# Copies with a factor, rotated products and raw latent tiles: out of PSUM by ScalarE or by VectorE

## The chip, the cores and the metric

The kernel runs on one core of a Trainium2 chip. Time is device time in microseconds; before the change the median of three runs is 1549.19 us (1547.57 to 1551.87). A separate execution was recorded by the hardware profiler, and all rows below come from it.

## The reference

A network of two different blocks, each of two layers, on 512 tokens of width 1024, all in float32. Cut to what matters:

```python
# block 1, each layer: h = x @ w_in, cut into the inputs of four branches
q  = rms_norm(c_q, q_norm) @ w_qb;  kv = rms_norm(c_kv, kv_norm) @ w_kvb      # mla: latents of rank 384 and 256
y_mla = softmax(causal(rope(q) k^T / sqrt(96))) v
y_sb  = stick_breaking(sq * d**-0.5, sk, sv)     # a[t,s] = sigmoid(z[t,s]) * prod_{s<j<t}(1 - sigmoid(z[t,j]))
y_fox = softmax(causal(fq * d**-0.5 . fk) + cumulated log forget gates) fv
y_mem = softmax((mem_q * d**-0.5) mk^T) mv                                    # keys and values from mem
merged = sum_n sigmoid(merge_r @ w_up)_n * ((y_n * silu(gate_n)) @ w_branch_n)
x = layer_norm(4**0.25 * x + merged @ w_out)
# block 2, each layer: h = rms_norm(x), z = h @ w_in_2, four attentions
q_a, k_a = axial_rope(rms_norm(q_a)), axial_rope(rms_norm(k_a))               # A: dense
q_b, k_b = rope(q_b), rope(k_b)                                               # B: window of 128, sink
o_c = neighbourhood(q_c, k_c, v_c, bias)                                      # C: 8x16 neighbourhood
q_d, k_d = rope(q_d), rope(k_d)                                               # D: difference of two softmaxes
x = x + concat(o_n * silu(g_n)) @ w_out_2
```

## The kernel before

There are five instruction streams (TensorE, VectorE, ScalarE, GpSimd, SyncE) that meet only at semaphores. A planner, `plan`, writes one list of steps. Each engine walks through the whole list in its order and takes from each step what is its own, so each engine's queue is the order of that list. A wait in a queue holds everything behind it on that engine.

**Matrix products.** Each is done in three passes for accuracy: a float32 operand is split into a high and a low part, and low x high, high x low and high x high are added in PSUM (L1399, L1400, L1401, one k-tile of 128 at a time). Weights of about 1 MB are loaded by DMA into one of two buffers, cast by ScalarE in pieces of 512 columns to the high part (L1552), and the low part is subtracted by VectorE (L1861) or GpSimd (L2296). The planner puts such a piece of the next weights in (`tick`) after every few k-tiles.

**Fill and main.** The planner interleaves two strands (`alongside`): the attention of one branch (main) and the projections of the next branch (fill). While mem's attention runs, mla's latents are projected; under mla's attention sb, under sb's fox, under fox's most of the merge. In the second block A is projected alone, then B under A's attention, D under B's, C under D's. So TensorE's order alternates between logits (L1421, L1427, L1439), transposes of the probabilities (L1455, L1464), probabilities times values (L1477), and k-tiles of projections.

**Attention.** Per chunk of two heads and 128 queries: logits into PSUM; VectorE takes the maximum (L2092, L2128) or adds the mask with it (L2105); ScalarE's exponential with the row sum (L1533, the line of a helper for every ACTIVATE with a function); TensorE transposes; the first half of the turned probabilities is copied by VectorE (L2165), the second by ScalarE (L1755); then the product with the values, the gate by VectorE (L2186), cast by ScalarE (L1767). The stick-breaking branch has sigmoids on ScalarE and scans and products on VectorE (L2151, L2154, L2157). D subtracts two softmaxes on VectorE (L2136 to L2141).

**Latents of mla.** Five tiles of 128 channels x 512 tokens (three of the query, two of the key and value latent) are computed, copied to SBUF raw (step `raw`, for the fourth `rawcopy`) by VectorE at L1958, and squared by ScalarE. TensorE sums the squares over channels (L1488), ScalarE makes the root (Ln, Exp), VectorE refines it by a Newton step (`newton_wide`, L1824 to L1830) and scales the tiles (L1968); ScalarE casts them (L1628), GpSimd makes the low part (L2310). The norm of the first three tiles (step `normed`) stands in the list behind the fifth tile's `raw`.

**Heads.** A branch that isn't rotated gets its queries by step `head` with part q: bank x 0.125 into SBUF, by VectorE at L1935, for fox in two halves of 64 partitions at L1932. There are two such steps (chunks c = 0, 1) per layer for each of mem, sb, fox and C. The keys (part k) are copied by ScalarE already (L1592, L1586).

**Rotated branches.** For A, B and D step `pair` copies each of three tiles (two of queries, one of keys) with its factor to SBUF (L2197 on VectorE; for A the factor is a column of gains). For A, ScalarE waits for this copy and then squares the same bank. Some k-tiles later TensorE multiplies the copy by a rotation matrix (L1508, step `rope2`), for A also the squares by a block of ones (L1516, step `qsquares`). VectorE combines copy and rotated product with the tables (L2208 to L2216), and for A refines the root and normalises (L1824 to L2224).

Of the kernel before, what the change touches and what calls it, by code (L numbers as in the profile page):

```python
# [1109 lines left out]
def build(nc, ctx, a, out):  # L1110
# [177 lines left out]
    def tensor_program(e):  # L1288
# [33 lines left out]
        def heads_ready(l, br):  # L1322
            if br == "mem":
                w.wait_ge(v_copy, v_copy.at(("head", l, br, "q", 1)))
                w.wait_ge(a_copy, a_copy.at(("mkv", l, 0, 1)))
                w.wait_ge(v_copy, v_copy.at(("mkv", l, 1, 1)))
            elif br == "mla":
                w.wait_ge(v_fn, v_fn.at(("rope1", l, "q")))
                w.wait_ge(v_copy, v_copy.at(("qnope", l, 1)))
                w.wait_ge(a_copy, a_copy.at(("mlav", l, 3)))  # L1330
            elif br in PAIRED:
                w.wait_ge(v_fn, v_fn.at(("paired", l, br, 2)))
                w.wait_ge(v_copy, v_copy.at(("vturn", l, br)))
            else:
                if br == "fox":
                    w.wait_ge(v_fn, v_fn.at(("foxrow", l, 3)))
                w.wait_ge(v_copy, v_copy.at(("value", l, br, 2)))
                w.wait_ge(a_copy, a_copy.at(("value", l, br, 3)))

        for s in STEPS:  # L1340
# [162 lines left out]
            elif k == "rope2":  # L1503
                b = s["b"]
                for g, v in b.free():
                    w.wait_ge(g, v)
                w.wait_ge(v_copy, v_copy.at(("pair", s["src"])))
                t = e.matmul(bank(b), C(ROT[s["br"]][0]), tm(s["src"]), start=True, stop=True)  # L1508
# [20 lines left out]
    def scalar_program(e):  # L1529
# [5 lines left out]
        for s in STEPS:  # L1535
# [37 lines left out]
            elif k == "spread":  # L1573
                for l in range(2):
                    w.wait_ge(d_z, d_z.at("z"))
                    src = zrow[:, l, :].unsqueeze(1).to_broadcast([60, 64, P])
                    e.dma_start(zscr[l], src).then_inc(d_spread.sem, d_spread.mark("z"))
            elif k == "head" and s["part"] == "k":
                l, br, c, b = s["l"], s["br"], s["c"], s["b"]
# [25 lines left out]
            elif k == "mkv" and s["n"] == 0:  # L1605
# [4 lines left out]
                t = e.copy(mk[:, c, :], bank(b)[:, 0:256])  # L1610
                t.then_inc(a_copy.sem, a_copy.mark(("mkv", l, 0, c), ends=(b,)))
            elif k in ("raw", "rawsquare"):
                w.wait_ge(v_copy, v_copy.at(("raw", s["l"], s["n"])))
                for g, v in s["tm"].free():
# [143 lines left out]
            elif k == "out":  # L1758
# [57 lines left out]
    def vector_program(e):  # L1816
# [35 lines left out]
        for s in STEPS:  # L1852
# [45 lines left out]
            elif k == "lambdas":  # L1898
# [10 lines left out]
                for l in range(2):  # L1909
# [9 lines left out]
                        v_fn.sem, v_fn.mark("lambdas"))  # L1919
            elif k == "head" and s["part"] == "q":  # L1920
                l, br, c, b = s["l"], s["br"], s["c"], s["b"]
                dst = QKV[br][0]
                w.wait_ge(gemm, gemm.at(b))
                if br in BEFORE:
                    w.wait_ge(heado, heado.at(("heado", l, BEFORE[br], 1)))
                if br == "sb":
                    w.wait_ge(y_lo, y_lo.at(("normed", l, 4)))
                if br == "fox":
                    w.wait_ge(p_fn, p_fn.at(("zeros", l)))
                    for half in range(2):  # L1930
                        p0 = 64 * half
                        t = e.tensor_scalar(dst[p0:p0 + 64, 2 * c + half, :], bank(b)[p0:p0 + 64, :], 0.125, None, ALU.mult)  # L1932
                        t.then_inc(v_copy.sem, v_copy.mark(("head", l, br, "q", c), ends=(b,)))
                else:
                    t = e.tensor_scalar(dst[:, c, :], bank(b), 0.125, None, ALU.mult)  # L1935
                    t.then_inc(v_copy.sem, v_copy.mark(("head", l, br, "q", c), ends=(b,)))
            elif k == "value" and s["i"] % 2 == 0:
# [11 lines left out]
            elif k == "mkv" and s["n"] == 1:  # L1949
# [5 lines left out]
                t.then_inc(v_copy.sem, v_copy.mark(("mkv", l, 1, c), ends=(b,)))  # L1955
            elif k in ("raw", "rawcopy"):
                w.wait_ge(gemm, gemm.at(s["b"]))
                t = e.tensor_copy(raw(s["n"]), bank(s["b"]))  # L1958
                t.then_inc(v_copy.sem, v_copy.mark(("raw", s["l"], s["n"]), ends=(s["b"],)))
            elif k == "normed":  # L1960
# [219 lines left out]
            elif k == "out":  # L2180
# [6 lines left out]
                t.then_inc(v_fn.sem, v_fn.mark(("gated", ta), ends=(b, s["u"])))  # L2187
            elif k == "pair":
                l, br, n, b = s["l"], s["br"], s["n"], s["b"]
                gain = 1.0 if n == 2 else {"A": None, "B": 0.125, "D": float(32 ** -0.5)}[br]  # L2190
                if br == "A":
                    gain = pcol(f"kna{l}") if n == 2 else qna8[:, l:l + 1]
                w.wait_ge(gemm, gemm.at(b))
                w.wait_ge(v_fn, v_fn.at("lambdas"))
                for g, v in s["tm"].free():
                    w.wait_ge(g, v)
                t = e.tensor_scalar(tm(s["tm"]), bank(b), gain, None, ALU.mult)  # L2197
                t.then_inc(v_copy.sem, v_copy.mark(("pair", s["tm"]), ends=(b,)))
            elif k == "rope2":
# [283 lines left out]
```

## Time and profile before

| | |
|---|---|
| median of three runs | 1549.19 us (1547.57 to 1551.87) |
| the profiled execution | 1553.94 us |
| its span | 1552.0 us, 21224 instructions |
| mean granted TensorE clock in it | 0.97 |
| moved copies, VectorE | 48 instructions: 12 of L1935, 8 of L1932, 10 of L1958, 18 of L2197 |

The span runs from the first to the last instruction of the profiled execution. A row of the time line has the start, the duration, the engine, the line, what is written from what; "[3.12 <-ACT prob L1755]" says that the engine had been idle for 3.12 us before this instruction and that the last thing it waited for was ScalarE's instruction at L1755. PE is TensorE, DVE VectorE, ACT ScalarE. Layers 0 and 1 of a block show the same pattern of waits, 416 to 426 us apart in the first block and 344 us in the second.

### The profile page before, as it was taken

The page shows a single profiled execution, that of the slowest core. Times are in us where ns is not written, and L with a number is a line of the kernel's source. Part 1 is how long each engine was busy: PE and PEld are TensorE (multiplying, and loading weights), DVE is VectorE, ACT ScalarE, POOL GpSimd, SP SyncE. Part 2 cuts the span into 40 slices and gives each one's busy share as a digit, 9 for nine tenths or more (in the row PEclk, how much of TensorE's full clock was granted, in tenths as well). Part 3 has the DMA queues.
Part 4 walks back from the last instruction along what each step waited for, and adds up shares of the span by engine and source line. Part 5 has one row for each costly group of instructions (what it writes and reads, how often), then busy time and mean ns, then how long its engine had stood idle before and what let it go on. Part 6 is the DMA issues. An engine that isn't in the chain of part 4 may idle for free.

```text
span 1552.0 us, 21224 instructions
## 1 busy us (share of the span) xinstructions
PE 1423.3 (92%) x8026; PEld 1097.0 (71%) x8026; DVE 904.6 (58%) x1705; ACT 681.2 (44%) x1477; POOL 366.7 (24%) x265
## 2 busy tenths in 40 slices
PE   7999898999989999999998699997999799997997
PEld 7757675877987576767788666665777656664776
DVE  4655437556672554484576565468655466568655
ACT  3544344555233554444552344335444444335443
POOL 2232121245231321222452111410001111310011
PEclk9999999999999999999999799999999899998999
DMA  6412620225333121211263323511213322511211
GB/s 225 109 29 85 158 68 28 62 61 204 109 136 82 29 82 55 82 35 56 67 224 85 93 54 68 116 55 48 93 64 96 82 63 60 116 55 48 96 62 54
DMA packets 191120, 131.72 MB, mean 85 GB/s; under 512 B 91436, under 2 KB 181164, under 8 KB 191020
## 3 DMA queue, kind: packets, MB, share of 16 engines
q1 hardware_dynamic: 179534, 112.29, 26.0%
q10 hardware_dynamic: 11486, 18.09, 3.6%
q8 instruction: 64, 1.05, 0.3%
q14 instruction: 36, 0.29, 0.1%
HBM read 118.03 MB, written 12.32 MB: 84 GB/s over the span
## 4 chain that ended last, share of the span: by engine, by line
PE 68%; DVE 18%; ACT 7%; issue 3%; DMA 2%; ACTq 1%; POOL 0%; DVEq 0%; POOLq 0%
PE pb L1399 18%; PE pb L1400 16%; PE pb L1401 16%; PE pb L1477 5%; PE pb L1421 5%; PE pb L1455 4%; ACT prob L1533 2%; DMA wr<-w_out 2%; ACT wh L1552 2%; ACT tmp L1533 1%; DVE wl L1861 1%; DVE scr L2151 1%; DVE xl L1868 1%; DVE small L2128 1%; PE pb L1439 1%
## 5 line engine op out<-in xcount | busy, mean ns | idle before, releaser
L2296 POOL TENSOR_TENSOR wl<-wr,wh 128x512 fp32r<-128x512 f32 x170 | 236.7, 1392 | 893.8 <-ACT wh L1552 890.1
L1399 PE MATMUL pb<-xh,wl 128*128 128x512 f32 (+1 forms) x832 | 354.0, 425 | 25.1 <-DVE xl L1868 21.9
L1400 PE MATMUL pb<-xl,wh 128*128 128x512 f32 (+1 forms) x832 | 323.6, 389 | 0.0
L1401 PE MATMUL pb<-xh,wh 128*128 128x512 f32 (+1 forms) x832 | 323.2, 388 | 0.0
L1861 DVE TENSOR_TENSOR wl<-wr,wh 128x512 fp32r<-128x512 f32 x200 | 162.9, 815 | 159.3 <-ACT wh L1552 159.0
L1399 PEld LDWEIGHTS pb<-xh,wl 128*128 128x128 f32 x832 | 164.0, 197 | 106.4 <-issue 54.1
L1552 ACT CAST wh<-wr 128x512 fp32r<-128x512 f32 x370 | 211.0, 603 | 50.2 <-PE pb L1401 42.8
L1401 PEld LDWEIGHTS pb<-xh,wh 128*128 128x128 f32 x832 | 163.5, 197 | 32.0
L1400 PEld LDWEIGHTS pb<-xl,wh 128*128 128x128 f32 x832 | 164.8, 198 | 24.3 <-issue 3.8
L1533 ACT ACTIVATE prob<-prob,small 128x512 f32<-128x512 f32 (+3 forms) x128 | 76.2, 597 | 153.0 <-DVE small L2105 143.6
L1455 PE MATMUL pb<-cst,prob 128*128 128x128 f32 x768 | 118.5, 276 | 24.4 <-ACT prob L1533 8.2
L1399 PE MATMUL pb<-wh,xl 128*128 128x256 f32 x448 | 130.9, 292 | 9.7 <-DVE xl L2047 3.6
L1455 PEld LDWEIGHTS pb<-cst,prob 128*128 128x128 f32 x768 | 94.0, 142 | 55.6 <-issue 14.6
L1400 PE MATMUL pb<-wl,xh 128*128 128x256 f32 x448 | 127.5, 285 | 0.0
L1401 PE MATMUL pb<-wh,xh 128*128 128x256 f32 x448 | 127.4, 284 | 0.0
L1533 ACT ACTIVATE tmp<-pb,cst 128x512 f32<-128x512 f32 (+3 forms) x116 | 74.3, 641 | 86.8 <-DVE tmp L2197 24.9
L1533 ACT ACTIVATE prob<-pb,small 128x512 f32<-128x512 f32 (+1 forms) x96 | 58.4, 612 | 113.8 <-DVE small L2092 60.8
L1399 PEld LDWEIGHTS pb<-wh,xl 128*128 128x128 f32 x448 | 86.5, 193 | 15.0 <-DVE xl L2047 4.4
L1755 ACT COPY prob<-pb 128x512 f32<-128x512 f32 (+3 forms) x128 | 61.4, 480 | 72.8 <-PE pb L1455 72.1
L1399 PE MATMUL pb<-wh,yl 128*128 128x256 f32 (+1 forms) x272 | 87.4, 321 | 2.5 <-DVE wl L1861 1.3
L1400 PEld LDWEIGHTS pb<-wl,xh 128*128 128x128 f32 x448 | 86.7, 193 | 0.7 <-issue 0.5
L1401 PEld LDWEIGHTS pb<-wh,xh 128*128 128x128 f32 x448 | 86.6, 193 | 0.0
(196 smaller groups left out, 2449.9 us busy)
## 6 DMA issues: line engine op xcount, KB each, us to landing
wr<-w_in SPq DMA_DIRECT2D x39, 1024.0 KB, 5.1
wr<-w_in SPq DMA_DIRECT2D x48, 256.0 KB, 4.6
wr<-w_out SPq DMA_DIRECT2D x10, 1024.0 KB, 5.7
wr<-w_branch SPq DMA_DIRECT2D x48, 128.0 KB, 2.3
x<-prob SPq DMA_DIRECT2D x12, 512.0 KB, 2.6
wr<-w_out SPq DMA_DIRECT2D x48, 128.0 KB, 3.0
wr<-w_mem_kv SPq DMA_DIRECT2D x4, 1024.0 KB, 5.5
prob<-x ACTq DMA_DIRECT2D x2, 2048.0 KB, 10.3
```

Source lines behind the costliest of these rows:

```text
L1399: e.matmul(ps, ll, rh, start=start, stop=False)
L1400: e.matmul(ps, lh, rl, start=False, stop=False)
L1401: t = e.matmul(ps, lh, rh, start=False, stop=stop)
L1421: t = e.matmul(bank(b)[:, 0:128 * (hi - lo)], lhs, rhs, start=True, stop=br != "mla")
L1439: t = e.matmul(bank(b), q_[rr, c, 128 * i:128 * i + 128], k_[rr, :], start=True, stop=True, tile_position=(32 * r, 0))
L1455: t = e.transpose(bank(b)[:, c], probs(p)[:, c], C("ident"))
L1477: t = e.matmul(bank(b)[64 * half:64 * half + 64, lo:hi], v_[:, j, vc:vc + 64], turns(s["t"][half])[:, j, lo - 256 * ih:hi - 256 * ih], sta ...
L1533: return e.activation(o, i, f, bias=C("zero", 0, i.shape[0]) if bias is None else bias, scale=scale, **kw)
L1552: e.copy(wh[:, j % 2, c0:c1], wr[:, j % 2, c0:c1]).then_inc(w_hi.sem, w_hi.mark((j, c)))
L1755: t = e.copy(turns(t_)[:, lo:hi, 128 * i:128 * i + 128], bank(b)[:, 0:128 * (hi - lo)].rearrange("p (j c) -> p j c", c=128))
L1861: t = e.tensor_tensor(wl[:, j % 2, c0:c1], wr[:, j % 2, c0:c1], wh[:, j % 2, c0:c1].bitcast(F32), ALU.subtract)
L2296: t = e.tensor_tensor(wl[:, j % 2, c0:c1], wr[:, j % 2, c0:c1], wh[:, j % 2, c0:c1].bitcast(F32), ALU.subtract)
```

## The change

The copies of three kinds of steps go from VectorE's program to ScalarE's, at the same place in the list of steps. Head copies with a factor become `e.mul` (0.125), raw latent tiles `e.copy`, the rotated branches' products an ACTIVATE with function Identity and the factor as its scale. All who waited for VectorE's copy now wait for ScalarE's. For `raw`, ScalarE copies, waits for its own copy and squares it; for A's `pair` it copies and then squares the same bank. The plan, its costs and the order of the steps stay as they are.

```diff
@@ tensor_program @@
             if br == "mem":
-                w.wait_ge(v_copy, v_copy.at(("head", l, br, "q", 1)))
+                w.wait_ge(a_copy, a_copy.at(("head", l, br, "q", 1)))
...
-                w.wait_ge(v_copy, v_copy.at(("pair", s["src"])))
+                w.wait_ge(a_copy, a_copy.at(("pair", s["src"])))
@@ scalar_program @@
+            elif k == "head" and s["part"] == "q":
+                l, br, c, b = s["l"], s["br"], s["c"], s["b"]
+                dst = QKV[br][0]
+                w.wait_ge(gemm, gemm.at(b))
...
+                if br == "fox":
+                    w.wait_ge(p_fn, p_fn.at(("zeros", l)))
+                    for half in range(2):
+                        p0 = 64 * half
+                        t = e.mul(dst[p0:p0 + 64, 2 * c + half, :], bank(b)[p0:p0 + 64, :], 0.125)
+                        t.then_inc(a_copy.sem, a_copy.mark(("head", l, br, "q", c), ends=(b,)))
+                else:
+                    t = e.mul(dst[:, c, :], bank(b), 0.125)
...
+            elif k == "rawcopy":
+                w.wait_ge(gemm, gemm.at(s["b"]))
+                t = e.copy(raw(s["n"]), bank(s["b"]))
...
             elif k in ("raw", "rawsquare"):
-                w.wait_ge(v_copy, v_copy.at(("raw", s["l"], s["n"])))
+                if k == "raw":
+                    w.wait_ge(gemm, gemm.at(s["b"]))
+                    t = e.copy(raw(s["n"]), bank(s["b"]))
+                    t.then_inc(a_copy.sem, a_copy.mark(("raw", s["l"], s["n"]), ends=(s["b"],)))
+                w.wait_ge(a_copy, a_copy.at(("raw", s["l"], s["n"])))
...
-            elif k == "pair" and s["br"] == "A":
-                w.wait_ge(v_copy, v_copy.at(("pair", s["tm"])))
+            elif k == "pair":
+                l, br, n, b = s["l"], s["br"], s["n"], s["b"]
+                gain = 1.0 if n == 2 else {"A": None, "B": 0.125, "D": float(32 ** -0.5)}[br]
+                if br == "A":
+                    gain = pcol(f"kna{l}") if n == 2 else qna8[:, l:l + 1]
+                w.wait_ge(gemm, gemm.at(b))
...
+                t = act(tm(s["tm"]), bank(b), ACT.Identity, gain)
+                t.then_inc(a_copy.sem, a_copy.mark(("pair", s["tm"]), ends=(b,)))
+                if br != "A":
+                    continue
@@ vector_program @@
-            elif k == "head" and s["part"] == "q":
...
-                    t = e.tensor_scalar(dst[:, c, :], bank(b), 0.125, None, ALU.mult)
...
-            elif k in ("raw", "rawcopy"):
...
-                t = e.tensor_copy(raw(s["n"]), bank(s["b"]))
...
-            elif k == "pair":
...
-                t = e.tensor_scalar(tm(s["tm"]), bank(b), gain, None, ALU.mult)
```

## Rows read from the trace of the kernel before

**Rows 1.** The page, busy time of three engines with share of the span.

```profile
PE 1423.3 (92%) x8026; PEld 1097.0 (71%) x8026; DVE 904.6 (58%) x1705; ACT 681.2 (44%) x1477; POOL 366.7 (24%) x265
```

**Rows 2.** TensorE's waits: for whom, us in total, times, longest.

```profile
PE pb L1399 <- DVE tmp L1830: 4.2, 4, 1.6
...
PE pb L1508 <- DVE tmp L2197: 1.9, 4, 0.6
```

**Rows 3.** Groups by line and shape: count, busy us, mean ns, idle before.

```profile
L2197 DVE TENSOR_SCALAR tmp<-pb 128x512 f32<-128x512 f32 x12 | 8.3, 692 | 4.0 <-PE pb L1401 4.0
...
L1533 ACT ACTIVATE tmp<-pb,cst 128x512 f32<-128x512 f32 x92 | 62.8, 683 | 74.7 <-DVE tmp L2197 24.9 <-PE pb L1421 13.5 <-PE pb L1401 13.0
...
L1543 ACT ACT_TABLE_LOAD x25 | 32.1, 1283 | 0.4
...
L1592 ACT COPY setB<-pb 128x512 f32<-128x512 f32 x8 | 4.6, 580 | 7.7 <-PE pb L1401 7.4
```

**Rows 4.** Time line, mla's latents in layer 0, VectorE and TensorE.

```profile
94.54 0.69 DVE L2186 SCALAR_TENSOR_TENSOR tmp<-pb,u 128x512 f32<-128x512 f32 x1 [1.81 <-PE pb L1477]
96.82 0.69 DVE L1958 COPY setB<-pb 128x512 f32<-128x512 f32 x1 [1.59 <-PE pb L1401]
97.43 1.80 DVE L1824 TENSOR_TENSOR scr<-tmp 128x512 f32<-128x512 f32 x1
...
103.17 0.42 DVE L2092 TENSOR_REDUCE small<-pb 128x1 f32<-128x256 f32 x1
...
106.67 0.33 PE L1455 MATMUL pb<-cst,prob 128*128 128x128 f32 x1 [0.73 <-DVE prob L2165]
...
108.79 0.67 DVE L1824 TENSOR_TENSOR scr<-tmp 128x512 f32<-128x512 f32 x1
...
113.89 1.55 PE L1477 MATMUL pb<-prob,tbias 128*64 128x256 f32 x6 [3.12 <-ACT prob L1755]
```

**Rows 5.** Time line, fox's first chunk of queries in layer 0.

```profile
244.11 1.41 DVE L1932 TENSOR_SCALAR setA<-pb 64x512 f32<-64x512 f32 x2 [3.58 <-PE pb L1401]
245.55 0.56 DVE L2165 COPY prob<-pb 128x384 f32<-128x384 f32 x1
...
250.53 0.52 PE L1455 MATMUL pb<-cst,prob 128*128 128x128 f32 x3 [1.29 <-DVE prob L2157]
```

**Rows 6.** Time line, fox's second chunk in layer 0, three engines.

```profile
255.32 1.40 DVE L1932 TENSOR_SCALAR setA<-pb 64x512 f32<-64x512 f32 x2
256.75 0.69 DVE L2186 SCALAR_TENSOR_TENSOR tmp<-pb,u 128x512 f32<-128x512 f32 x1
...
257.48 0.62 ACT L1767 CAST yh<-tmp 128x512 fp32r<-128x512 f32 x1 [5.18 <-DVE tmp L2186]
...
259.71 1.65 PE L1421 MATMUL pb<-setB 64*128 64x384 f32 x4 [2.38 <-ACT prob L1533]
...
262.31 0.63 PE L1401 MATMUL pb<-xh,wh 128*128 128x512 f32 x1
...
263.37 0.40 PE L1401 MATMUL pb<-xh,wh 128*128 128x512 f32 x1
```

**Rows 7.** Table by stretches: busy us of each engine, clock, DMA share, GB/s.

```profile
259.70:262.90 3.20, 3.19 (x8) 1.83 (x9) 2.25 (x6) 1.56 (x5) 0.00 (x0) 0.50 0.00 0
```

**Rows 8.** Time line, A's second and third tile in layer 0.

```profile
899.51 0.74 DVE L2197 TENSOR_SCALAR tmp<-pb,qna 128x512 f32<-128x512 f32 x1
...
900.28 0.69 ACT L1533 ACTIVATE tmp<-pb,cst 128x512 f32<-128x512 f32 x1 [3.86 <-DVE tmp L2197]
...
914.96 0.50 PE L1399 MATMUL pb<-xh,wl 128*128 128x512 f32 x1 [0.50 <-DVE tmp L1830]
```

**Rows 9.** Time line, C's first chunk of queries in layer 0.

```profile
1075.31 0.69 DVE L1861 TENSOR_TENSOR wl<-wr,wh 128x512 fp32r<-128x512 f32 x1 [0.97 <-ACT wh L1552]
...
1076.65 0.65 PE L1477 MATMUL pb<-prob,setA 128*64 128x256 f32 x4 [0.20 <-DVE prob L2165]
```

**Rows 10.** Time line, ScalarE behind B's first product in layer 0.

```profile
948.01 0.62 ACT L1767 CAST yh<-tmp 128x512 fp32r<-128x512 f32 x1 [3.75 <-DVE tmp L2186]
```

More of the change, by code:

```diff
@@ L1577, in scalar_program @@
                     e.dma_start(zscr[l], src).then_inc(d_spread.sem, d_spread.mark("z"))
-            elif k == "head" and s["part"] == "k":
+            elif k == "head" and s["part"] == "q":
+                l, br, c, b = s["l"], s["br"], s["c"], s["b"]
+                dst = QKV[br][0]
+                w.wait_ge(gemm, gemm.at(b))
+                if br in BEFORE:
+                    w.wait_ge(heado, heado.at(("heado", l, BEFORE[br], 1)))
+                if br == "sb":
+                    w.wait_ge(y_lo, y_lo.at(("normed", l, 4)))
+                if br == "fox":
[6 more added lines that the diff above has]
+                    t = e.mul(dst[:, c, :], bank(b), 0.125)
+                    t.then_inc(a_copy.sem, a_copy.mark(("head", l, br, "q", c), ends=(b,)))
+            elif k == "head":
                 l, br, c, b = s["l"], s["br"], s["c"], s["b"]
@@ L1611, in scalar_program @@
                 t.then_inc(a_copy.sem, a_copy.mark(("mkv", l, 0, c), ends=(b,)))
+            elif k == "rawcopy":
+                w.wait_ge(gemm, gemm.at(s["b"]))
+                t = e.copy(raw(s["n"]), bank(s["b"]))
+                t.then_inc(a_copy.sem, a_copy.mark(("raw", s["l"], s["n"]), ends=(s["b"],)))
             elif k in ("raw", "rawsquare"):
-                w.wait_ge(v_copy, v_copy.at(("raw", s["l"], s["n"])))
+                if k == "raw":
+                    w.wait_ge(gemm, gemm.at(s["b"]))
+                    t = e.copy(raw(s["n"]), bank(s["b"]))
+                    t.then_inc(a_copy.sem, a_copy.mark(("raw", s["l"], s["n"]), ends=(s["b"],)))
+                w.wait_ge(a_copy, a_copy.at(("raw", s["l"], s["n"])))
                 for g, v in s["tm"].free():
@@ L1767, in scalar_program @@
                 e.copy(yh[:, s["yc"] + c, :], tm(s["ta"])).then_inc(a_hi.sem, a_hi.mark(("out", l, br, c)))
-            elif k == "pair" and s["br"] == "A":
-                w.wait_ge(v_copy, v_copy.at(("pair", s["tm"])))
+            elif k == "pair":
[4 more added lines that the diff above has]
+                w.wait_ge(gemm, gemm.at(b))
+                w.wait_ge(v_fn, v_fn.at("lambdas"))
+                for g, v in s["tm"].free():
+                    w.wait_ge(g, v)
+                t = act(tm(s["tm"]), bank(b), ACT.Identity, gain)
+                t.then_inc(a_copy.sem, a_copy.mark(("pair", s["tm"]), ends=(b,)))
+                if br != "A":
+                    continue
                 for g, v in s["sq"].free():
@@ L1919, in vector_program @@
                         v_fn.sem, v_fn.mark("lambdas"))
-            elif k == "head" and s["part"] == "q":
[L1921 to L1934, printed above, removed]
-                    t = e.tensor_scalar(dst[:, c, :], bank(b), 0.125, None, ALU.mult)
-                    t.then_inc(v_copy.sem, v_copy.mark(("head", l, br, "q", c), ends=(b,)))
             elif k == "value" and s["i"] % 2 == 0:
@@ L1955, in vector_program @@
                 t.then_inc(v_copy.sem, v_copy.mark(("mkv", l, 1, c), ends=(b,)))
-            elif k in ("raw", "rawcopy"):
-                w.wait_ge(gemm, gemm.at(s["b"]))
-                t = e.tensor_copy(raw(s["n"]), bank(s["b"]))
-                t.then_inc(v_copy.sem, v_copy.mark(("raw", s["l"], s["n"]), ends=(s["b"],)))
             elif k == "normed":
@@ L2187, in vector_program @@
                 t.then_inc(v_fn.sem, v_fn.mark(("gated", ta), ends=(b, s["u"])))
-            elif k == "pair":
[L2189 to L2196, printed above, removed]
-                t = e.tensor_scalar(tm(s["tm"]), bank(b), gain, None, ALU.mult)
-                t.then_inc(v_copy.sem, v_copy.mark(("pair", s["tm"]), ends=(b,)))
             elif k == "rope2":
```

## The prediction

> **What bounds the kernel now.** I read the page first. TensorE is busy 92% of the 1552.0 us span, VectorE 58%, ScalarE 44% [rows 1]. Taking copies from VectorE is therefore worth nothing by itself: it counts only where TensorE stands still and VectorE's queue is the reason. So the second view is the list of TensorE's waits. It adds up to about 119 us, most of it elsewhere (input, layer norms, the stick-breaking scans). Directly behind a moved copy stand only four short waits, 1.9 us together [rows 2]. The rest has to be looked for in the time line: at each of the 48 moved instructions I asked what its engine does next, what it did while TensorE waited, and when the matmuls that feed it had ended. Last comes the table by stretches, for TensorE's clock.
>
> **What one copy costs.** On VectorE a moved copy of 128x512 takes 0.69 us, with a per-partition factor 0.75; two halves of 64 partitions take 1.40 to 1.41 [rows 3, 5, 6, 8]. ScalarE's plain copies of the same shape from PSUM take 0.58, its ACTIVATE with a bias column 0.68 [rows 3]. The head copies and raw tiles become plain copies or multiplications by an immediate: I take 0.59. The 18 rotated products become ACTIVATE with a bias column: 0.69. The six of branch A have a column as factor too, which no row shows; the bounds are 0.58 (the copy) and 0.78 (0.68 and once more the 0.10 that separates the two forms), I take 0.74 and the difference decides nothing below. In all, VectorE loses 33.5 us of work (42 x 0.69 and 6 x 0.75) and ScalarE gains 30.3 (22 x 0.59, 8 x 0.58, 12 x 0.69, 6 x 0.74). Of each nothing but the following counts.
>
> The Trainium skill speaks against the change: its page "ScalarE: Activation LUTs" (Rules for kernel authors) sends a multiplication to VectorE and not to ScalarE. For float32 out of PSUM the rows say the opposite, 0.58 against 0.69. By the rule's order each copy would be no shorter after the move, which takes nothing from the gains below (they come from the queue, not from the length) and raises the loss by 0.1 a site.
>
> **Part 1, the raw latent tiles (10 copies): gain.** Four of five per layer come while VectorE or ScalarE waits for TensorE anyway, and the Square behind each starts at the same moment as before: it waited for VectorE's 0.69, now for ScalarE's 0.59 and the engine's own semaphore. The fifth is different. At 96.82 it stands in VectorE's queue ahead of the norm of the query latent (L1824 to L1968) and waits for the fifth tile's matmuls, although the root that the norm needs was ready at 89.6. VectorE's last work before it ended at 95.2 [rows 4]. Without it the norm starts at 95.2 and not 97.43, and the logits' maxima behind it (L2092, at 103.17, while those logits were ready at 98.8) come 2.2 us earlier, if not 3.3: L1824's 1.80 there has a usual 0.67, the rest being a stall beside GpSimd. Then TensorE's wait of 0.73 at 106.67 goes. What is late next: the second norm starts at 108.79 behind the maxima and L2165 [rows 4]; these now follow TensorE's squares and logits that end at 105.9, so maxima until 106.9, L2165 until 107.3, norm at 107.35. The root is ready by 106.8. That is 1.44 earlier, and it is this norm that ScalarE's casts and then L1755 wait for, and for which TensorE stands 3.12 us until 113.89 [rows 4]. So the point of 113.89 comes 1.44 earlier, and once more in layer 1, where the same pattern stands at 539.74: **2.9 us**. Bounds: 0 (the norm turns out held by GpSimd's subtractions or ScalarE) and 2.2 a layer.
>
> **Part 2, head copies.** Those of mem (4) and sb (4) are free: ScalarE waits for TensorE before what follows them, for 1.9 us and more each time, and so did VectorE. The cover of mem's is the 8.7 us in which ScalarE waits for the weight buffer; a cast then starts 0.6 late, for weights needed 14 us on.
> fox, first chunk: its two halves hold VectorE from 244.11 to 245.52, and L2165, whose transposes were done at 245.0, starts at 245.55. From there VectorE runs without a gap to the product that TensorE waits 1.29 for at 250.53 [rows 5]. Gain 0.5. ScalarE has finished a cast at 244.1 and needs about 1.1 for both halves, to 245.25; its next work waits for transposes until 245.44. A cover of only 0.2 us.
> fox, second chunk: the matmuls ended at 253.2, VectorE copies at 255.32 after its scans, and L2186, whose product was done at 254.9, starts only at 256.75. ScalarE has idled 5.18 us for it; then come its cast, four sigmoids, and TensorE, after 2.38 us, at 259.71 [rows 6]. With the copies on ScalarE at 253.3 to 254.4, in its idle time, L2186 starts at 255.43: gain 1.3, and TensorE still waits 1.1. Together **3.6 us** in two layers; bounds 0 and 2 x 2.4.
> C, first chunk: here VectorE's queue is not the limit, ScalarE's is. After four exponentials ScalarE casts weights at 1074.65; VectorE idles 0.97 for that cast, then L1861, L2165 and TensorE, which waits 0.20, at 1076.65 [rows 9]. The copy comes between the exponentials and the cast: all of it 0.59 later, and VectorE runs without a gap to the next two stalls, so nothing takes it back. Second chunk: VectorE idles over 1 us for transposes behind it, free. **Loss 1.2 us** in two layers (0 to 2 x 1.2).
>
> **Part 3, rotated products (18 copies).** In B and D ScalarE idles for at least 1.2 us behind the first two of three (3.75 before its next work at B's first [rows 10]); behind the third, two casts come 0.7 later, for weights that are not the next ones. Nothing gained, nothing lost. In A VectorE is the engine that is late: the copies of tiles two and three start straight behind the previous tile's norm, about 2.4 us after their matmuls ended, while ScalarE idles 3.86 and 4.03 for them [rows 8]. Moved, they finish before TensorE asks: 0.38 and 0.58 a layer, just the four waits of [rows 2]. Behind the third tile TensorE waits 0.50 for L1830 at 914.96 [rows 8]; that norm starts when ScalarE's root is ready and not behind VectorE's backlog, 0.3 earlier. **2.5 us** in two layers; bounds 1.9 and 2.9.
>
> **TensorE's clock.** From 259.70 to 262.90 the granted clock is 0.50, so 1.2 GHz, and matmuls of 0.40 us take 0.63; before it TensorE had waited 2.38 us [rows 6, 7]. Waits of 1.29 to 1.42 (250.53 among them) had no such stretch behind them. With 1.1 us left of the wait the slow stretch should go, in both layers: 3.2 us of work at half speed, 1.6 us each, **3.2 us**. Behind 113.89 the wait shrinks from 3.12 to 3.12 - 1.44 + 0.73 = 2.4, as long as the one that slowed the clock, so nothing is booked.
>
> **The sum.** 2.9 + 3.6 + 2.5 - 1.2 = 7.8 us, with the clock 11.0. The profiled execution took 1553.9 us around its 1552.0 us span; it would take 1542.9. The median of the timed runs is 1549.19, 4.7 below the profiled one, and the same 11.0 come off it: **1538.2 us**.
>
> **The rivals.**
> - The queue gains hold and the clock does not care: slow stretches move to other waits instead. For it speaks that two waits of 1.28 and 1.02 close together, with none over 2 us, are also followed by a slow one. 1549.2 - 7.8 = 1541.4 us.
> - Relief of the wrong engine: the norms and scans are held by GpSimd or by ScalarE's root, so that parts 1 and 2 give a quarter and only A's four waits go. For it: L1824's 1.80 and a 1.30 for an L2154 of usually 0.27 just ahead of fox's second chunk. Against: both chains show VectorE without a gap. 6.5 / 4 + 1.9 - 1.2 = 2.3, so 1546.9 us: no change that can be told.
> - Slower: ScalarE's queue becomes the limit inside the attentions, as at C's first chunk. Its queue is in order, and behind each copy stand a weight cast, exponentials or L1755, for which VectorE's L1861, then L2165, then TensorE wait. 28 copies lie there: 12 of B and D at 0.69, 8 of sb and C at 0.59, fox's 8 halves at 0.58, 17.6 us. It decides where ScalarE's idle time behind the copy is shorter than the copy; the rows give 1.2 to 5.2 us nearly everywhere, which speaks against it. If half were paid and parts 1 and A still gave 5.4: 1549.2 + 8.8 - 5.4 = 1552.6; if all and fox's gain lost, 1561.
> - The copies are not what they seem: the Identity form makes ScalarE reload its function table. The page of the profile charges 1.28 us for a load and has 28 of them [rows 3]; two more for each of 18 products would be 46 us, 1595 us. Plain copies run between loads without any. The Trainium skill, "ScalarE: Activation LUTs" (Table sets: the hidden batching unit), says that identity and copy lie in every set; no row shows Identity.
>
> **How the numbers follow.** Forecast 1538.2: 0.50; clock indifferent, 1541.4: 0.20; wrong engine, 1546.9: 0.18; slower by ScalarE's queue: 0.10; table loads: 0.02. About 0.3%, 4.6 us, is what a measurement here can tell from no change. The first two cases and 0.02 of the third are faster, 0.72; the rest of the third and a little of the slower case can't be told from no change, 0.17; slower 0.11. The low end: all upper bounds of parts 1 to 3 add 5 us, of which half is believable, and the slow stretch behind 113.89 may shorten: 1532. The high end takes in the third case: 1549.
>
> **What would show it.** Right: L1824 starts before the fifth raw tile is copied; TensorE's wait for L1755 near 113 is 2.4 and not 3.1; the wait at 259.7 near 1.1 with the clock at 1.00 behind it; no wait of L1508 left; VectorE near 871 and ScalarE near 711 us; TensorE's wait for L2165 near 1076 about 0.8. Wrong: waits of TensorE for ScalarE's exponentials or of L1861 for the cast that grow at the heads of fox or the products of B and D; more than 28 table loads; slow clock stretches at places that had none.

## The result and the profile after

The changed kernel took **1537.7 us** (median of 4 runs, 1534.9 to 1539.4) against 1549.3 (4 runs): ratio 0.9918, 95% interval 0.9900 to 0.9936. Later runs of the same 48 moved copies gave 0.9919 (0.9902 to 0.9935). It is faster by 0.8%, and the forecast was 1538.2 us.

The profiled execution of after took 1534.9 us around a span of 1533.1; that of before 1553.9 around 1552.0. The two spans differ by 19 us and the medians by 12. Single executions of one kernel differ by several us, so no single pair of traces gives the size of the gain; the sections below use three profiles of each.

The page of the kernel after, answering to [rows 1]. VectorE and ScalarE came out within 1.5 us of what was forecast (871 and 711):

```profile
PE 1413.1 (92%) x8026; PEld 1091.0 (71%) x8026; DVE 869.9 (57%) x1657; ACT 709.6 (46%) x1525; POOL 366.7 (24%) x265
```

TensorE's waits after (for whom, us in total, times, longest), answering to [rows 2]. The waits of the next rotation (now L1516) for the copies of A's products are no longer in the list. Those for ScalarE's copy L1780 (mla) and its exponentials at L1421 (fox) have shrunk; one for L2180 (branch C) has grown to 0.7:

```profile
PE pb L1477 <- ACT prob L1780: 5.4, 6, 2.1
...
PE pb L1421 <- ACT prob L1533: 4.8, 4, 1.4
PE pb L1399 <- DVE tmp L1866: 4.4, 4, 1.6
...
PE pb L1477 <- DVE prob L2180: 1.4, 2, 0.7
```

The groups of ScalarE by line and shape (count, busy us, mean ns, idle before), answering to [rows 3]: the moved copies' own durations. The multiplications take 0.592 and 0.597, the raw tile's copy 0.585; the products with a number as factor went into the group of 0.684 (104 where there were 92); those with a column as factor take 0.782, the upper bound that was given. The count of table loads is the same 25:

```profile
L1533 ACT ACTIVATE tmp<-pb,cst 128x512 f32<-128x512 f32 x104 | 71.1, 684 | 61.5 <-PE pb L1401 17.3 <-PE pb L1421 13.5 <-PE pb L1516 11.7
...
L1543 ACT ACT_TABLE_LOAD x25 | 32.1, 1283 | 0.4
...
L1593 ACT ACTIVATE setB<-pb 128x512 f32<-128x512 f32 x12 | 7.2, 597 | 16.8 <-PE pb L1401 16.8
...
L1590 ACT ACTIVATE setA<-pb 64x512 f32<-64x512 f32 x8 | 4.7, 592 | 2.1 <-PE pb L1401 1.9
L1636 ACT COPY setB<-pb 128x512 f32<-128x512 f32 x8 | 4.7, 585 | 9.1 <-PE pb L1401 9.1
...
L1533 ACT ACTIVATE tmp<-pb,cst,qna 128x512 f32<-128x512 f32 x4 | 3.1, 782 | 9.1 <-PE pb L1401 9.1
```

The time line of mla's latents in layer 0, answering to [rows 4]. Times are 2.2 us earlier than before from the kernel's first 45 us on, which some other profiles of the unchanged kernel show too: this part of the difference between the two spans is not the change. The norm of the query latent (L1860 on) now starts at 92.99, straight behind L2201, while the fifth raw tile is copied by ScalarE at 94.67. GpSimd's subtraction at 95.25 now falls on L1864 and L1866, which take 1.02 and 1.65 where 0.43 and 0.69 are usual; before, one of 1.28 at 97.40 fell on L1824. TensorE waits 2.10 where it waited 3.12, and the wait of 0.73 ahead of it is gone:

```profile
92.99 0.68 DVE L1860 TENSOR_TENSOR scr<-tmp 128x512 f32<-128x512 f32 x1
...
94.44 1.02 DVE L1864 TENSOR_SCALAR scr<-scr 128x512 f32<-128x512 f32 x1
94.67 0.59 ACT L1636 COPY setB<-pb 128x512 f32<-128x512 f32 x1 [0.41 <-PE pb L1401]
95.25 1.34 POOL L2300 TENSOR_TENSOR wl<-wr,wh 128x512 fp32r<-128x512 f32 x1
95.49 1.65 DVE L1866 TENSOR_TENSOR tmp<-tmp,scr 128x512 f32<-128x512 f32 x1
...
104.83 0.68 DVE L1860 TENSOR_TENSOR scr<-tmp 128x512 f32<-128x512 f32 x1
...
109.94 1.08 PE L1477 MATMUL pb<-prob,tbias 128*64 128x256 f32 x8 [2.10 <-ACT prob L1780]
```

The time lines of fox, A and C in layer 0, answering to [rows 5, 6, 8, 9]. Fox's first wait is 0.88 and was 1.29; ScalarE copies the second chunk at 247.83, L2201 follows the scans at 249.88, and TensorE waits 1.05 and not 2.38. A's third wait is 0.57 (0.50 before). In C the head copy (1054.93) stands between the exponentials and the cast at 1055.41; VectorE waits 2.05 for that cast and TensorE 0.68:

```profile
245.09 0.63 PE L1455 MATMUL pb<-cst,prob 128*128 128x128 f32 x4 [0.88 <-DVE prob L2172]
247.83 1.21 ACT L1590 ACTIVATE setA<-pb 64x512 f32<-64x512 f32 x2 [0.97 <-PE pb L1401]
249.88 0.68 DVE L2201 SCALAR_TENSOR_TENSOR tmp<-pb,u 128x512 f32<-128x512 f32 x1
...
252.96 0.92 PE L1421 MATMUL pb<-setB 64*128 64x384 f32 x4 [1.05 <-ACT prob L1533]
...
895.03 0.50 PE L1399 MATMUL pb<-xh,wl 128*128 128x512 f32 x1 [0.57 <-DVE tmp L1866]
...
1054.93 0.61 ACT L1593 ACTIVATE setB<-pb 128x512 f32<-128x512 f32 x1
1055.41 0.64 ACT L1552 CAST wh<-wr 128x512 fp32r<-128x512 f32 x1
...
1056.08 0.69 DVE L1897 TENSOR_TENSOR wl<-wr,wh 128x512 fp32r<-128x512 f32 x1 [2.05 <-ACT wh L1552]
...
1057.43 1.95 PE L1477 MATMUL pb<-prob,setA 128*64 128x256 f32 x16 [0.68 <-DVE prob L2180]
```

Table by stretches after, answering to [rows 7]: behind fox's wait the clock is 1.00 in both layers, behind mla's 0.70 in layer 0 and 1.00 in layer 1. (Columns: PE, PEld, DVE, ACT, POOL busy, clock, DMA share, GB/s.)

```profile
252.90:256.20 3.30, 3.24 (x14) 2.32 (x15) 2.20 (x6) 2.39 (x6) 0.00 (x0) 1.00 0.03 5
658.90:662.20 3.30, 3.30 (x15) 2.33 (x16) 2.14 (x6) 2.39 (x7) 0.00 (x0) 1.00 0.00 0
109.90:113.30 3.40, 3.36 (x14) 2.51 (x15) 0.69 (x1) 2.21 (x3) 3.24 (x3) 0.70 0.05 11
526.10:529.50 3.40, 3.40 (x19) 2.27 (x21) 0.69 (x1) 2.18 (x4) 3.24 (x3) 1.00 0.02 4
```

### The profile page after: what moved, and what is told of

It reads as the page before. It is cut to its first block, busy times and chain, and to the rows that moved or that the text cites. A ratio compares the mean times of both kernels' runs of the same rounds, so it can differ in the third digit from the quotient of the medians.

```text
span 1533.1 us, 21207 instructions
## 1 busy us (share of the span) xinstructions
PE 1413.1 (92%) x8026; PEld 1091.0 (71%) x8026; DVE 869.9 (57%) x1657; ACT 709.6 (46%) x1525; POOL 366.7 (24%) x265
## 3 DMA queue, kind: packets, MB, share of 16 engines
q8 instruction: 64, 1.05, 0.3%
## 4 chain that ended last, share of the span: by engine, by line
PE 69%; DVE 17%; ACT 8%; issue 3%; DMA 1%; ACTq 1%; POOL 0%; DVEq 0%; POOLq 0%
PE pb L1399 18%; PE pb L1400 16%; PE pb L1401 16%; PE pb L1477 6%; PE pb L1421 5%; PE pb L1455 4%; ACT prob L1533 3%; ACT wh L1552 2%; ACT tmp L1533 1%; DVE wl L1897 1%; DVE small L2143 1%; DVE prob L2156 1%; DVE xl L1904 1%; DVE scr L2166 1%; DMA wr<-w_out 1%
## 5 line engine op out<-in xcount | busy, mean ns | idle before, releaser
L1399 PE MATMUL pb<-xh,wl 128*128 128x512 f32 (+1 forms) x832 | 350.9, 422 | 25.5 <-DVE xl L1904 21.9
L1399 PEld LDWEIGHTS pb<-xh,wl 128*128 128x128 f32 x832 | 162.0, 195 | 103.7 <-issue 50.1
L1399 PE MATMUL pb<-wh,xl 128*128 128x256 f32 x448 | 130.0, 290 | 8.0 <-DVE xl L2062 3.5
L1455 PEld LDWEIGHTS pb<-cst,prob 128*128 128x128 f32 x768 | 95.2, 143 | 54.3 <-issue 14.6
L1533 ACT ACTIVATE tmp<-pb,cst 128x512 f32<-128x512 f32 (+3 forms) x128 | 82.6, 645 | 71.2 <-PE pb L1421 21.4
L1399 PEld LDWEIGHTS pb<-wh,xl 128*128 128x128 f32 x448 | 85.7, 191 | 13.0 <-DVE xl L2062 4.3
L1780 ACT COPY prob<-pb 128x512 f32<-128x512 f32 (+3 forms) x128 | 61.4, 480 | 69.3 <-PE pb L1455 68.3
L1399 PE MATMUL pb<-wh,yl 128*128 128x256 f32 (+1 forms) x272 | 87.4, 321 | 2.5 <-DVE wl L1897 1.3
L2180 DVE COPY prob<-pb 128x512 f32<-128x512 f32 (+3 forms) x128 | 70.5, 551 | 31.3 <-PE pb L1455 30.8
```

The lines of the kernel that those rows point to most:

```text
L1399: e.matmul(ps, ll, rh, start=start, stop=False)
L1455: t = e.transpose(bank(b)[:, c], probs(p)[:, c], C("ident"))
L1533: return e.activation(o, i, f, bias=C("zero", 0, i.shape[0]) if bias is None else bias, scale=scale, **kw)
L1780: t = e.copy(turns(t_)[:, lo:hi, 128 * i:128 * i + 128], bank(b)[:, 0:128 * (hi - lo)].rearrange("p (j c) -> p j c", c=128))
L2180: t = e.tensor_copy(turns(t_)[:, lo:hi, 128 * i:128 * i + 128], bank(b)[:, 0:128 * (hi - lo)].rearrange("p (j c) -> p j c", c=128))
```

## The experiments

Ten kernels are one program with a switch. Each of the 48 copies stands in both engines' programs, and a table says which engine does it; everything else is the changed kernel (in two of the ten one transfer is later as well). Line numbers in their rows are 17 to 62 higher than those of before (L1494 is L1477, L1438 is L1421, L1526 is L1508, L1416 is L1399).

```diff
+MOVED = {"head": lambda l, br, c: ..., "raw": lambda l, n: ..., "pair": lambda l, br, n: ...}
+def on_scalar(s):
+    if s.kind == "head": return s["part"] == "k" or MOVED["head"](s["l"], s["br"], s["c"])
+    if s.kind in ("raw", "rawcopy"): return MOVED["raw"](s["l"], s["n"])
+    return MOVED["pair"](s["l"], s["br"], s["n"])
```

### None moved, and all moved, again

```diff
 e2_none, e12_none_again:  head, raw, pair -> False
 e1_all, e13_all_again:    head, raw, pair -> True
```

Expected of none: 

> None of the 48 copies moved: the kernel before again, to get a second profiled execution of it. The first one spanned 1552.0 us with 96.4 us of slow clock (granted 0.50) in it, the changed kernel's 1533.1 us with 79.0. Theory (the change is worth about 11 us, and the other 7 us between the two spans are a difference of single executions): this span lies between 1544 and 1552 us, and at least one of the slow stretches that the changed kernel's trace lacks for no visible reason (389.4, length 3.4 us; second half of the one at 112.9; 539.6) is absent here too, while the two behind fox's wait (259.7 and 676.1) are there. Rival (every one of the slow stretches hangs on the place of the waits, and the whole 18.9 us belong to the change): the span is 1552 again, with the same stretches. Ratio to the kernel before 1.000 by both.

Of all: 

> All 48 copies moved: the changed kernel again, for its interval and a second profiled execution. Theory: ratio 0.9925 (11.6 us less), span between 1533 and 1539 us, the clock behind fox's wait (near 253 and 659) at 1.00 again. Rival (the clock's gain behind fox was luck of one execution): one or both of the stretches at 0.50 are back, the ratio nearer 0.995 (7.8 us less).

Of the third profile of none: 

> No copy moved, a third profile of the kernel before. Theory (what differs between the profiles of the two kernels near 385 belongs to the kernel): w_out's transfer lands 14.5 us after its issue again, TensorE waits 1.6 us near 385. Rival (it varies from one execution to the next): it lands after 12 to 13.5 us and the wait is under 0.6 us. The clock: at least one of the stretches of half speed behind fox's two waits of 2.4 us is there.

And of all: 

> All 48 copies moved, a third profile. Theory: w_out's transfer lands 12.4 us after its issue, no wait near 375, and no stretch at half clock behind fox's two waits of 1.05 us. Rival: it lands after 13.5 us or more and TensorE waits over 0.5 us there.

Measured: none 0.9993 (0.9979 to 1.0007), span 1549.6; all 0.9919 (0.9902 to 0.9935), span 1534.9. The third profiles span 1547.8 and 1538.1. So three spans of the one average 1549.8 and of the other 1535.4. That the first pair's 19 us were partly chance is shown. The place that I had named for it was wrong: all three slow stretches that I expected to see go in the second profile of none (near 389, 113 and 540) were there again, and what the first pair differs by for no reason of the change is elsewhere, 2.2 us of it in the first 45 us. The late transfer and the wait near 385 came in all three profiles of none and in none of the three of all, with these landing times of w_out in the third profiles (KB each, us from issue to landing), first none, then all:

```profile
wr<-w_out SPq DMA_DIRECT2D x1, 1024.0 KB, 14.8
```

```profile
wr<-w_out SPq DMA_DIRECT2D x1, 1024.0 KB, 12.5
```

In the third profile of none ScalarE waits 2.04 for it and TensorE 1.85, five us later:

```profile
375.06 1.14 ACT L1570 CAST wh<-wr 128x512 fp32r<-128x512 f32 x2 [2.04 <-DMA wr<-w_out]
...
380.57 0.35 PE L1416 MATMUL pb<-wh,xl 128*128 128x256 f32 x1 [1.85 <-POOL wl L2358]
```

This is a gain of 1.6 to 1.85 us in the traces that my sum did not have. From the issue of this transfer to that of the third w_out behind it, it takes 30.0 to 30.2 us in the profiles of none and 28.1 in those of all. The trace of before showed the wait, and I had not asked what the waits far behind the moved copies would do.

### Only the fifth raw tile, only fox's second chunk, only A's products, only the rest

```diff
 e3_raw5:   raw  -> n == 4                      (2 copies)
 e4_fox2:   head -> br == "fox" and c == 1      (4 halves)
 e5_pairA:  pair -> br == "A"                   (6 copies)
 e8_rest:   head -> br in ("mem", "sb") or br == "C" and c == 1;  raw -> n < 4;  pair -> br in ("B", "D")
```

Raw tile: 

> Only the fifth raw latent tile of each layer moved (two copies). Theory (part 1: it stood ahead of the norms in VectorE's queue): TensorE's wait near 113.9 falls from 3.1 to 2.1 us in both layers and the one of 0.73 near 106.7 goes, 1.8 us a layer, so 3.6 us; where the slow stretches of the clock behind the two waits shorten as in the kernel with all moved, up to 3.4 us more. Time 3.6 to 7 us below that of the kernel before, ratio 0.9977 to 0.9955. Rival (the norms are held by GpSimd): under 1 us, ratio 0.9995. Beside it, a stretch that my prediction did not book: in the kernel before the weight transfer of w_out issued near 365 takes 14.6 us to land, ScalarE's cast waits 2.0 for it and TensorE 1.74 near 385.5; with all moved it lands after 12.3 and that wait is gone. If that hangs on the first layer's mla, it is gone here.

Measured 0.9959 (0.9947 to 0.9971), 6.4 us. The theory holds and GpSimd as holder of the norms does not. The waits of 0.73 and 3.1 became nothing and 2.1 in both layers, just as with all moved. That is 3.5 of the 6.4 us. For the rest there are two candidates, which this kernel does not separate: the wait near 385 is gone in its profile, and the mean clock of its timed runs is higher, 0.9726 against 0.9709 of before on the same chip. TensorE's waits with this kernel:

```profile
109.94 1.08 PE L1494 MATMUL pb<-prob,tbias 128*64 128x256 f32 x8 [2.10 <-ACT prob L1803]
...
526.74 1.08 PE L1494 MATMUL pb<-prob,tbias 128*64 128x256 f32 x8 [2.13 <-ACT prob L1803]
```

Fox: 

> Only fox's second chunk of queries moved (four halves). Theory (part 2 and the clock): TensorE's wait near 259.7 falls from 2.4 to 1.05 us in both layers, 1.3 us each, and the stretch at half clock behind it (3.4 us, costing 1.7) goes: 2.6 + 3.4 = 6.0 us, ratio 0.9961. Rival 1 (the clock does not care): 2.6 us, ratio 0.9983. Rival 2 (the norms behind are held by something else): 0. If w_out's transfer near 365 hangs on fox's copies, its wait of 1.74 is gone here too, up to 3.4 us more with the slow stretch behind it.

Measured 0.9982 (0.9969 to 0.9995), 2.8 us. The waits fell as forecast, and the clock behind both is 1.00 in this profile:

```profile
254.04 0.92 PE L1438 MATMUL pb<-setB 64*128 64x384 f32 x4 [1.07 <-ACT prob L1551]
...
663.80 0.92 PE L1438 MATMUL pb<-setB 64*128 64x384 f32 x4 [1.06 <-ACT prob L1551]
```

```profile
254.00:257.40 3.40, 3.36 (x15) 2.42 (x16) 2.17 (x6) 2.49 (x7) 0.00 (x0) 1.00 0.00 0
663.80:667.20 3.40, 3.40 (x15) 2.44 (x16) 2.13 (x6) 2.49 (x7) 0.00 (x0) 1.00 0.00 0
```

But the time is that of rival 1, the waits alone, although the wait near 385 is gone in this profile too. The mean clock over its 12 timed runs is 0.9709 against 0.9707 over 69 of before; two stretches of 3.4 us less would have made it 0.0022 higher. That speaks against a net gain from the clock here, at two standard errors.

A: 

> Only branch A's rotated products moved (six copies). Theory (part 3: VectorE is the late engine there): the four waits of the next rotation for them (0.38 and 0.58 a layer) go, and the whole is worth 1.4 us a layer as the stretch measured with all moved, 2.8 us, ratio 0.9982. Rival (the gain there came from earlier work, not from these copies): 0 to 1 us. Nothing near 385 is expected to change, as A comes later.

Measured 0.9991 (0.9980 to 1.0002), 0.5 us by the medians and 1.3 by the means, and no difference that the times alone can tell. The trace can: the two waits for the copies are gone, and from one common wait near 874.2 to the third tile's it takes 36.6 us and not 37.9, 1.3 a layer. All of it is at the two copies. An idle time is counted from the end of the matmul before, which lasts 0.39 us, while in a stream the next one starts 0.23 behind its start; so a wait listed as 0.39 puts the next start off by 0.54 (0.77 against 0.23 at the first copy), and that of 0.57 by 0.73. The mean clock of these runs is lower than that of before on the same chip, 0.9695 against 0.9709; compared at equal clock (0.9 us per 0.001, see the end) they are 2.5 us faster, standard error 0.5, as the trace has it. TensorE, first none moved, then A's:

```profile
896.71 0.39 PE L1418 MATMUL pb<-xh,wh 128*128 128x512 f32 x1
897.48 1.13 PE L1526 MATMUL pb<-tmp,cst 128*128 128x512 f32 x2 [0.39 <-DVE tmp L2259]
...
905.51 1.13 PE L1526 MATMUL pb<-tmp,cst 128*128 128x512 f32 x2 [0.57 <-DVE tmp L2259]
...
912.13 0.50 PE L1416 MATMUL pb<-xh,wl 128*128 128x512 f32 x1 [0.50 <-DVE tmp L1892]
```

```profile
896.73 0.39 PE L1418 MATMUL pb<-xh,wh 128*128 128x512 f32 x1
896.96 1.02 PE L1526 MATMUL pb<-tmp,cst 128*128 128x512 f32 x2
...
910.84 0.50 PE L1416 MATMUL pb<-xh,wl 128*128 128x512 f32 x1 [0.56 <-DVE tmp L1892]
```

The rest: 

> Moved are the copies to which the prediction gave nothing: mem's and sb's heads, C's second chunk, the first four raw tiles of each layer and the products of B and D (30 copies). Theory: 0, ratio 0.999 to 1.001. Rival (ScalarE's queue: each of them delays what stands behind it): up to 30 x 0.6 = 18 us slower, a quarter of it 4.5 us, ratio 1.003. Other rival (they bring what the sum left out: w_out's late transfer near 365 and the slow stretch behind it): 1.7 to 3.4 us faster, ratio 0.998.

Measured 0.9982 (0.9970 to 0.9995), 1.4 us less by the medians and 2.2 by the means. The rival "ScalarE's queue" falls: these 30 copies, 18 of which it had counted (B, D, sb, C's second), cost nothing that the runs can tell. The other rival, a gain that the sum left out, fits: in its profile w_out lands after 12.3 us and near 385 only the wait for VectorE is left, which was there before:

```profile
385.59 0.39 PE L1416 MATMUL pb<-wh,xl 128*128 128x256 f32 x1 [1.18 <-DVE xl L2109]
```

### Branch C's first chunk, alone and left out

```diff
 e7_C1:    head -> br == "C" and c == 0;  raw, pair -> False
 e6_noC1:  head -> not (br == "C" and c == 0);  raw, pair -> True
```

Alone: 

> Only branch C's first chunk of queries moved. Theory: 0.5 to 0.6 us lost in each layer at TensorE's wait for VectorE's product near 1076.6 (0.20 becomes about 0.7), so 1.2 us slower, ratio 1.0007. Rival: 0, ratio 1.000. Faster is expected by neither.

Left out: 

> All moved but branch C's first chunk of queries (one copy a layer), which stays on VectorE. Theory (the copy stands between ScalarE's exponentials and the cast that VectorE's L1897 waits for): TensorE's wait for L2180 near 1057 falls from 0.68 back to 0.2 us in both layers, and the time is 1.0 to 1.2 us below that of the kernel with all moved, ratio 0.9918 where that has 0.9925. Rival (VectorE takes the 0.6 us back in a later stall): the same as with all moved.

Measured: alone 1.0013 (1.0000 to 1.0027), 2.0 us slower; left out 0.9906 (0.9887 to 0.9925), 1534.7 us against 1538.4 for all moved on the same chip. The sign is as forecast both times. The waits are the cause: 0.67 and 0.66 alone, 0.20 and 0.21 left out. Alone, then left out:

```profile
1071.91 1.95 PE L1494 MATMUL pb<-prob,setA 128*64 128x256 f32 x16 [0.67 <-DVE prob L2227]
...
1418.77 1.52 PE L1494 MATMUL pb<-prob,setA 128*64 128x256 f32 x12 [0.66 <-DVE prob L2227]
```

```profile
1055.79 1.95 PE L1494 MATMUL pb<-prob,setA 128*64 128x256 f32 x16 [0.20 <-DVE prob L2227]
...
1401.53 1.95 PE L1494 MATMUL pb<-prob,setA 128*64 128x256 f32 x16 [0.21 <-DVE prob L2227]
```

Two waits longer by 0.47 are 0.9 us. Both measured values are above that, and neither excludes it: alone the interval runs from 0 to 4.2 us, and left out the means differ by 1.9 with a standard error of 1.3.

### The late transfer, taken apart

In none moved, and in the best kernel so far (all but C's first chunk), one transfer of the group that ScalarE issues near 366 is issued later (the wait for its buffer moves with it):

```diff
             elif k == "xload":
...
-                    t = e.dma_start(memt, a["mem"][0].rearrange("(t p) c -> p t c", p=P))
...
             elif k == "merged":
...
+                if not l and m == 5:
...
+                    t = e.dma_start(memt, a["mem"][0].rearrange("(t p) c -> p t c", p=P))
```

None moved: 

> No copy moved; one transfer later: the 1 MB of the memory input for layer 1 is issued by ScalarE ahead of the sixth merged tile (near 384) and not near 366, among the 4 MB that it issues there. Theory (w_out's transfer of 1 MB shares the 16 engines with these 4 MB and so lands 14.6 us after its issue; ScalarE waits 2 us for it, VectorE 2.5 for that cast, TensorE 1.6 to 1.7 near 385): with 3 MB it lands 11 to 12 us after its issue, the wait near 385 is gone, and the stretch at half clock behind it (1.7 us of cost) with it: 1.6 to 3.4 us less than the kernel before, ratio 0.9989 to 0.9978. Rival (w_out is late for another reason): lands after 14 us or more, no change. A price would be a wait of TensorE for the memory input near 411: 0 expected.

All but C's first: 

> All copies moved but branch C's first chunk, and the memory input issued later as in the other kernel. Theory (with the copies moved w_out's transfer lands after 12.4 us anyway and nobody waits for it): the same as the kernel without C's first chunk, 1534.7 to 1536 us, ratio 0.9906. Rival (the late landing happens in some executions of that kernel too): up to 1.5 us faster than it.

Measured: 1.0001 (0.9986 to 1.0015) and 0.9920 (0.9897 to 0.9942). In the first, w_out lands after 12.5 us, the wait near 385 is gone and none comes near 411. In the other the wait was not there before, w_out lands after 12.3 us where it was 12.4, and the time is no better; the ratio of 0.9906 that was expected lies in the interval. The landing with none moved:

```profile
wr<-w_out SPq DMA_DIRECT2D x1, 1024.0 KB, 12.5
```

That the 4 MB have a part in the lateness is not shown by this: seven profiles in which all 4 MB are there land after 12.3 to 12.7 us as well. Taking the wait away brought nothing that the 12 times show. But the mean clock of these runs is 0.9690, lower than the 0.9707 of before. Compared at equal clock (0.9 us per 0.001, the slope over all runs of this study) they are 1.1 us faster than all 80 runs of none moved and 1.6 faster than before on the same chip, with a standard error of 0.5, and in the trace the stretch from w_out's issue to the third one behind it takes 28.0 us, as with all moved. Whether the lower clock is chance or a price of the edit no run shows, so in plain time what the wait near 385 is worth stays open between 0 and 1.8 us.

## Why the prediction was right, and where it was not

The total was right, and the terms of its parts 1 to 3 were confirmed one by one. What it missed, up to 1.8 us a term, cancels in part, so that the total came within 0.5 us of the median is in part luck. "Found" is for both layers, from TensorE's waits in three profiles of either kernel unless said otherwise.

| Step of the prediction | forecast | found |
|---|---|---|
| Part 1, raw tile ahead of the norms | 2.9 | 3.5 |
| Part 2, fox, first chunk | 1.0 | 0.8 |
| Part 2, fox, second chunk | 2.6 | 2.7 |
| mem, sb, B, D, first four raw tiles, C's second chunk | 0 | 0 |
| Part 2, C's first chunk | -1.2 | -1.0 (timed alone: -2.0) |
| Part 3, A | 2.5 | 2.6 |
| Wait near 385, one layer | not seen | 0 to 1.8 |
| TensorE's clock | 3.2 | 1.7 to 3.2 |
| Sum | 11.0 | 10.3 to 13.6; timed 12.4 |

The timed value compares 10 runs of all moved (1538.0 us, mean) with 80 of none moved (1550.4). Compared at equal clock (0.9 us per 0.001) the difference is 10.7 us, standard error 0.5; the rows of the table without the clock's add up to 8.6, and to 10.4 with the wait near 385 at its full 1.8, so this speaks for that wait being worth most of what it lasted. The separate kernels (raw tile, fox, A, C, the rest) add up to 11.4 us by the differences of their means from before on the same chip (standard error 2.6), and to 13.2 against the 80 runs, without fox's first chunk but with the vanished wait near 385 in three of them; so no large gain or loss hangs on moving them together.

- **Part 1** held in its mechanism and was 0.3 a layer too small. I let the second norm start at 107.35 behind the maxima; less the 2.2 by which this execution is early that is 105.15, and it came at 104.83. The wait that I put at 2.4 is therefore 2.10.
- **Part 2, fox and C** held in place, order and size: L2201 no longer waits behind the copy, the wait of 1.1 is there, C's wait is 0.68 where 0.8 was said.
- **Part 3** held in size; a quarter of it is not where I put it. The wait for L1866 did not fall by 0.3 but grew from 0.50 to 0.57, and the whole pattern comes 1.3 earlier all the same: from start to start of the matmuls the two copies held TensorE up by 0.54 and 0.73, and not by the 0.38 and 0.58 of the idle times that I added.
- **The clock** is the weakest step. At the place named it came out: behind fox's second wait of 2.4 the granted clock fell to 0.50 (1.2 GHz) in 13 of 16 cases (8 profiles of kernels that have this wait, two layers), behind the wait of 1.05 in none of 12. But "should go, in both layers" took for certain what the wait only makes likely. With none moved, the third profile has 1.00 behind the first wait and 0.53 behind the second:

```profile
256.20:259.60 3.40, 3.36 (x15) 2.43 (x16) 2.28 (x6) 2.50 (x7) 0.00 (x0) 1.00 0.00 0
672.20:675.60 3.40, 3.40 (x11) 2.06 (x8) 1.75 (x6) 2.55 (x6) 0.00 (x0) 0.53 0.00 0
```

  And I booked nothing behind mla's wait because 2.4 was "as long as the one that slowed the clock". There the time at half clock fell from 8.5 us a profile (8 profiles, both layers) to 4.5 (6 profiles). Together the two places would make the mean clock 0.003 higher; the timed runs say 0.0019 (0.9726 over 10 runs, 0.9707 over 80, standard error 0.0006), so part of it is lost again at other places. Twice the missing share times the time is 90.7 us at half clock against 84.2, so 3.2 us of TensorE's work at most; by the slope over all runs (below) it is 1.7. The rival that the clock does not care (7.8 us, 1541.4) is refuted in its time for the whole change, not in its idea that slow stretches move: fox's kernel alone behaved like that.
- **Not in the sum:** the wait near 385. It stood in the kernel before as the longest of two waits for GpSimd's L2296, 1.7 us, and no moved copy is near it.
- **ScalarE's queue, the slower rival,** costs nothing outside C that a run shows: the 18 such copies in the kernel of the rest and fox's second chunk came without a loss, and fox's first chunk, with its cover of only 0.2 us, was moved only together with all others, where the wait behind it fell as forecast. **Relief of the wrong engine** is refuted by the raw tile's kernel. **Table loads** stayed at 25; the 28 that the prediction names are a misreading, the row has 25 before as well. The Trainium skill, "ScalarE: Activation LUTs" (Table sets: the hidden batching unit), has identity and copy in every set, and this trace agrees. Its rule that a multiplication belongs to VectorE (Rules for kernel authors) gives its reason for bf16; for float32 out of PSUM it is 0.597 on ScalarE against 0.692 on VectorE here.

The best kernel is all moved but C's first chunk: 11 runs with and without the later transfer average 1536.8 us, 1.1 below all moved, with a standard error of 0.8.

## What to carry to other kernels

A copy taken from an engine that is not the bottleneck is worth what its place in the queue held up, not its length: 2 of the 48 copies (the fifth raw tiles) gave half of the gain when moved alone, 3.5 us of it by the waits that they had held up, 30 gave nothing at their own places, and 2 cost 1 to 2 us. So ask for each moved instruction what stands behind it on the old engine and on the new one, and leave out those where the new queue feeds the late chain. And look for waits that end on a transfer just after the changed stages too: they change with the rest, even if nobody touches them.

## What the runs showed of the hardware

- **One transfer, two landing times.** w_out's 1 MB, issued 0.15 us ahead of ScalarE's 4 MB, lands after 14.5 to 14.8 us in all profiles of none moved and of C's first chunk alone, after 13.4 with A's copies alone, and after 12.3 to 12.7 in the nine others (two of them with 3 MB beside it). Where a program has three profiles, none moved and all moved, it keeps to the program and not to the execution. The others have one profile each; A's copies, whose stage comes 500 us later, may shift it or that execution may be an exception. The cause is open. The traffic of the 30 us around it in the kernel before, by queue (packets, MB, share of the engines), q10 being ScalarE's:

```profile
q10 hardware_dynamic: 1088, 4.19, 35.8%
q1 hardware_dynamic: 2496, 2.88, 29.7%
```

  That is 3.9 KB and 1.15 KB a packet. The Trainium skill, "DMA: Bandwidth & Descriptors" (Queues, rings and completion order), says that each engine takes whole packets from its queues in turn. An estimate by that, if the packets of the profile are those that it means, which no run shows: 1 MB of small packets lands with 3.3 MB of the large ones, 4.3 MB at the measured 0.4 MB per us, 11 us and about 1 to start. This agrees with 12.4; for 14.6 it gives no reason.
- **VectorE beside GpSimd.** 0.43 became 1.02 and 0.69 became 1.65 next to a GpSimd subtraction of 1.34 us; moving VectorE's work earlier only chose another victim. The Trainium skill, "GPSIMD Engine Reference" (1. Specifications), names the SBUF interface that the two share and VectorE's instructions with two SBUF inputs as those that contend for it; L1866 is one, and the trace agrees (1.65 for 0.69). L1864 has one SBUF input and was stretched as well (1.02 for 0.43); why, no run here shows.
- **Clock and time.** Within the runs of one kernel, taken over all 165 runs of the study, 0.001 of mean granted clock goes with 0.9 us, which is two thirds of the variance between executions of one kernel (1543 to 1555 us with none moved).
